# Modulation panels moved from attention's in-projection to the last layer's DeltaNet core

## The reference, cut to what matters

```
for i in range(DEPTH):
    m_ctx = split(silu(c_ctx) @ ada_w[i] + ada_b[i], 6)     # ada_w[i]: 1024 x 6144
    m_lat = split(silu(c) @ ada_w[i] + ada_b[i], 6)
    h = modulate(x, norm_mix[i], m[0], m[1])
    x = x + m[2] * mixer_i(h)
    h = modulate(x, norm_ffn[i], m[3], m[4])
    x = x + m[5] * channel_mixer_i(h)
```

## Time and profile before

| | |
|---|---|
| median of 3 runs | 2366.56 us (2366.43 to 2367.58) |
| profiled execution | 2363.55 us |
| its span, first to last instruction | 2361.7 us |
| PE busy | 2241.4 us, 95% |
| DVE busy | 483.8 us, 20% |
| ACT busy | 393.0 us, 17% |
| modulation matmuls (768) | 98.1 us |
| mean granted TensorE clock | 0.972 |

### The profile page before, as it was taken

One profiled execution on the slowest core, in us unless ns is written; L12 is line 12 of the kernel. 1 busy time (PEld: TensorE's weight loads), 2 busy tenths in 40 slices (PEclk: granted clock), 3 DMA queues, 4 the chain that ended last, 5 costly groups with the idle time before them and its releaser, 6 DMA issues.

```text
span 2361.7 us, 43842 instructions
## 1 busy us (share of the span) xinstructions
PE 2241.4 (95%) x19531; PEld 1614.3 (68%) x19531; DVE 483.8 (20%) x1376; ACT 393.0 (17%) x819; POOL 66.9 (3%) x109
## 2 busy tenths in 40 slices
PE   6999998999999999899998899999998889998999
PEld 4776666888888655445676588888878875454455
DVE  2234332000112400000211410002344423000002
ACT  1133223000100100000113310002143331000001
POOL 4000001000000000000000000000000000000000
PEclk8999999999999899999999899999999999999999
DMA  8967898753356499999574695414440057999991
GB/s 326 275 232 286 314 318 268 210 155 116 107 169 210 151 384 387 380 379 382 211 241 170 225 277 177 134 36 125 132 136 7 12 178 256 386 382 379 379 387 51
DMA packets 355909, 550.90 MB, mean 233 GB/s; under 512 B 11280, under 2 KB 311184, under 8 KB 343232
## 3 DMA queue, kind: packets, MB, share of 16 engines
q1 hardware_dynamic: 344352, 525.31, 64.1%
q0 software_dynamic: 5840, 18.11, 3.0%
q10 hardware_dynamic: 5536, 4.73, 0.6%
HBM read 537.64 MB, written 14.93 MB: 234 GB/s over the span
## 4 chain that ended last, share of the span: by engine, by line
PE 85%; DVE 5%; DMA 3%; SPq 3%; ACT 2%; issue 1%; ACTq 0%; DVEq 0%
PE ps L641 83%; SPq L481 3%; DMA ring<-in_moe_w_down 2%; ACT ring L1441 1%; DVE ring L1989 1%; ACT work L1441 1%; DVE ring L2007 0%; DVE work L1848 0%; PE ps L1137 0%; DVE ring L2012 0%; DVE ring L1997 0%; PE ps L1032 0%; DMA ring<-in_ada_w 0%; DVE ring L2015 0%; PE ps L667 0%
## 5 line engine op out<-in xcount | busy, mean ns | idle before, releaser
L641 PE MATMUL ps<-ring,work 128*32 128x384 f32 (+6 forms) x7752 | 700.7, 452 | 36.7 <-DMA ring<-in_moe_w_down 26.0
L641 PE MATMUL ps<-hT,ring 128*128 128x256 f32 x3200 | 714.6, 382 | 3.4 <-DVE hT L1858 3.2
L641 PEld LDWEIGHTS ps<-hT,ring 128*128 128x128 f32 x3200 | 609.4, 191 | 113.3 <-issue 12.2
L641 PEld LDWEIGHTS ps<-ring,work 128*32 128x32 f32 (+2 forms) x7752 | 340.5, 116 | 371.7 <-issue 257.0
L1441 ACT ACTIVATE work<-ps 128x256 f32<-128x256 f32 (+5 forms) x244 | 101.8, 436 | 1350.7 <-PE ps L641 1170.5
L641 PE MATMUL ps<-work,ring 128*128 128x256 f32 (+1 forms) x1344 | 289.7, 375 | 10.9 <-DVE work L2074 6.3
L641 PEld LDWEIGHTS ps<-work,ring 128*128 128x128 f32 (+1 forms) x1344 | 243.0, 188 | 47.3 <-DVE work L2074 8.0
L641 PE MATMUL ps<-ring 64*64 64x64 f32 (+1 forms) x4192 | 183.2, 230 | 18.6 <-ACT ring L1441 7.2
L641 PEld LDWEIGHTS ps<-ring 64*64 64x64 f32 x4192 | 160.7, 139 | 58.0 <-ACT ring L1441 24.2
L1441 ACT ACTIVATE ring<-ps 128x512 f32<-128x512 f32 (+3 forms) x208 | 101.6, 491 | 341.0 <-PE ps L641 329.9
L641 PE MATMUL ps<-work 128*128 128x128 f32 (+2 forms) x736 | 107.4, 297 | 4.3 <-DVE work L2194 4.2
(11 more groups left out here) (263 smaller groups left out, 948.9 us busy)
## 6 DMA issues: line engine op xcount, KB each, us to landing
ring<-in_moe_w_gu SPq DMA_DIRECT2D x96, 1536.0 KB, 16.0
ring<-in_ada_w SPq DMA_DIRECT2D x96, 1024.0 KB, 7.1
ring<-in_moe_w_down SPq DMA_DIRECT2D x48, 1536.0 KB, 16.1
ring<-in_ff_w_gu SPq DMA_DIRECT2D x88, 512.0 KB, 6.0
ring<-in_dn_w_in SPq DMA_DIRECT2D x32, 1024.0 KB, 5.4
ring<-in_moe_w_gu SPq DMA_DIRECT2D x32, 1024.0 KB, 8.8
ring<-in_ff_w_down SPq DMA_DIRECT2D x44, 512.0 KB, 7.3
ring<-in_moe_w_down SPq DMA_DIRECT2D x32, 512.0 KB, 11.6
```

Source lines behind the costliest of these rows:

```text
L641: return pe.matmul(out, lhsT, rhs, start=start, stop=stop, **kw)
```

## The change

Layer 2's in-projection gets no modulation panels. Its loop over heads keeps 16, now of groups 9 and 10. The last eight (group 11, the last third of layer 3's modulation) are computed in layer 3's own core: five behind `s_ks` of pair 0, one at place x = 3 in each of pairs 1 to 3, and the turn behind level 1 of pair 3. The sequences, and so the slots, follow.

```
-EARLY, GATES, CORE, NA_IN, NA_GATES = 8, 16, 48, 8, 16
+EARLY, GATES, CORE, NA_GATES, LATE = 8, 16, 48, 16, 8
...
     if KIND[l] == "na":
-        late = ada[EARLY + GATES + CORE:]
-        mixed = []
-        for i, u in enumerate(units):
-            mixed.append(u)
-            if 1 <= i <= NA_IN:
-                mixed.append(late[i - 1])
-        units = mixed + late[NA_IN:]
+        units += ada[EARLY + GATES + CORE:-LATE]
+    if l == DEPTH - 1:
+        units += ada[-LATE:]
     return units + [("out", i) for i in range(4)]
...
+        PANELS3 = [{1: 5}, {3: 1}, {3: 1}, {3: 1}]
...
                 def s_ks(j):
-                    if j == 0 or l == 0:
-                        pe.wait_ge(d_ar, ada_turned[0])
+                    pe.wait_ge(d_ar, ada_turned[0])
...
                 def s_z(j):
-                    if l == 0:
-                        pe.wait_ge(d_ar, ada_turned[0])
+                    pe.wait_ge(d_ar, ada_turned[0])
...
                 def panels(j, x):
-                    for _ in range(PANELS[j].get(x, 0) if l == 0 and j < PAIRS else 0):
+                    for _ in range((PANELS if l == 0 else PANELS3)[j].get(x, 0) if j < PAIRS else 0):
                         ada(0)
-                def turn(j, when):
-                    if l == 0 and j in when:
+                def turn(j, when, late):
+                    if (l == 0 and j in when) or (l > 0 and j in late):
                         pe.wait_ge(d_r0, head(l, j, 1)[2] + 1)
                         ada_turn(ZB, ROWS512(l, True))
...
                         if lev in (1, 3):
-                            turn(j, TURN_UT1 if lev == 1 else TURN_UT3)
+                            turn(j, TURN_UT1 if lev == 1 else TURN_UT3, (3,) if lev == 1 else ())
...
             def attention(l):
                     project(u[w], w % 2, hT, 2 * l if w == 0 else None)
-                    if 1 <= w <= NA_IN:
-                        ada(2, 3, ROWS512(l))
-                ada_turn(3, ROWS512(l))
...
-                    out(j, OUT_QD)
+                    out(j, OUT_QD, (3,))
...
-                            turned(j, TURN_UT1)
+                            turned(j, TURN_UT1, (3,))
...
-                ada_rows(2, ROWS512(l))
-                modulation(3)
```

More of the change, by code:

```diff
@@ L316, in trunk @@
         assert sum(sum(x.values()) for x in PANELS) == CORE
+        PANELS3 = [{1: 5}, {3: 1}, {3: 1}, {3: 1}]
+        assert sum(sum(x.values()) for x in PANELS3) == LATE
         PJ0 = {0: 0, 1: 12, 2: 20, 3: 32}
@@ L2034, in both, with out, turned @@
                         step(*head(l, j, p))
-                def out(j, when):
-                    if l == 0 and j in when:
+                def out(j, when, late=()):
+                    if (l == 0 and j in when) or (l > 0 and j in late):
                         ada_rows(0, ROWS512(l, True))
-                def turned(j, when):
-                    if l == 0 and j in when:
+                def turned(j, when, late=()):
+                    if (l == 0 and j in when) or (l > 0 and j in late):
                         modulation(ZB)
```

## The result

| | before | changed |
|---|---|---|
| median | 2366.49 us (2361.10 to 2367.58, 6 runs) | 2352.82 us (2351.50 to 2357.81, 6 runs) |
| profiled execution | 2363.55 us | 2353.04 us |
| span | 2361.7 us | 2351.2 us |
| mean granted TensorE clock | 0.972 | 0.978 |

The ratio is 0.9949 (95% interval 0.9936 to 0.9962): 12 us less, between 9 and 15. Two more comparisons of the same two kernels gave 0.9959 (0.9947 to 0.9971) and 0.9961 (0.9947 to 0.9975), about 9.5 us less. The profiled executions differ by 10.5.

The account below looks back on a forecast made before the run. TensorE's order of work was taken to bound the kernel (85% of the chain). -8.93 - 0.44 - 2.1 + 1.0 + 0.4 = -10.1 us gave 2356.5 from a median of 2366.56; range 2353.5 to 2361.0.

Parts of the forecast that it names:

- panels and turn out of layer 2's in-projection: Layer 2's in-projection is TensorE-bound, so removing eight panels saves 8.93 us and the turn's four transposes 0.44.
- core, pair 0: clock kept: Layer 3's core: five panels hold the granted clock, returning 0.77 + 1.36 = 2.1 us; lower bound 0.
- core, pair 0: five panels: Layer 3's core, behind s_ks: panels fit under the vector engine's time and cost nothing; 4.5 us without that cover.
- core, x = 3, three times: Pairs 1 to 3, between s_t of head 0 and s_tz: one panel each costs 0.34 us, 1.0 for three.
- core, the turn: Pair 3 behind level 1: four transposes, 0.66 us in layer 0, partly under a 0.23 us ScalarE wait, cost 0.4.
- my three panels: Layer 2's in-projection: three weight panels without modulation panels between take 20.82 us, 6.94 each, used to price the saving.
- The lower price of 0.97 for each panel: Layer 2's in-projection: a modulation panel alone takes 0.97 us, giving only 7.8 saved, the lower bound to 8.93.
- The cover of pair 0: Layer 3's core: the vector engine sets the 7.61 us from s_ks to s_t of head 1; five panels fit under it.
- the equality of 7.61 in both layers: s_ks to s_t of head 1 takes 7.61 us in layer 0 with five panels and in layer 3 without.
- The caution that I took from the same page: The gate's phase is free, slow matmuls vary between runs, so the 2.1 us is uncertain; without it the gain is 8.0.
- Transfers: The eight 1 MB loads, issued as layer 3's slots free, and the output panels behind them land in time: hidden.
- The first expert's weights: Their stream ends some 9 us earlier but waits, since the next expert's first load awaits the first gate product: nothing.

Follow-up runs that it names:

- with six: Changed kernel with loads apart, six panels in pair 0's hole, none in pair 3, the turn behind the core; ratios 0.9966 and 0.9964 against the kernel before.
- the kernel with the hole filled: Kernel before plus 40 panel-shaped matmuls on constants behind s_ks of pair 0 in layer 3's core, result unused, no loads; ratio 0.9993, pair 0 27.78 us.
- the late panels left out: Changed kernel without group 11's eight panels, their loads, copy, turn and addition, ones in place of their results; ratio 0.9967 against the kernel before.
- the hole left open: Changed kernel with pair 0's five panels moved to place 3 of pair 1, so six stand there; ratio 0.9987 against the kernel before.
- loads apart: Changed kernel with the seventh and eighth late panel loads held to pairs 1 and 2, output panels to the core's tail; ratios 0.9938 and 0.9943.
- the execution with held-back loads: Kernel before, hole open, with four output panels and two first-expert loads (7 MB) waiting for s_ks of pair 0; pair 0 33.15 us, not 29.97.

## Why the prediction was right, point by point

The forecast was 2356.5 us from a median of 2366.56, 10.1 less. The measured median, 2352.8, lies 0.7 below the low end of my range; the ratio times 2366.56 gives 2354.5, inside it. By the traces ("the sums" are the few 512-column matmuls that add up squares for a norm, one such step ahead of layer 2's heads and one at the end of the core, ahead of layer 3's output projection):

| term | forecast | measured |
|---|---|---|
| panels and turn out of layer 2's in-projection | -9.37 | -9.79 |
| core, pair 0: clock kept | -2.1 | -2.2 |
| core, pair 0: five panels | 0 | 0 |
| core, pair 0: stall by the burst of loads | not in the sum | +1.7 |
| core, x = 3, three times | +1.0 | +0.7 |
| core, the turn | +0.4 | +0.64 |
| clock in the sums ahead of layer 2's heads, and in those at the end of the core | not in the sum | -0.4, -0.95 |
| sum of the rows | -10.1 | -10.3 |

The spans differ by 10.5; the 0.2 that the rows leave is spread over stages that weren't edited. That the total came out so near is luck in part: the stall of 1.7, which I had not foreseen, is made good by 1.35 of clock that I had not foreseen either, and by 0.4 more from layer 2.

**Layer 2.** Right in kind: TensorE set this stage and what left it came off. It was 0.4 more, since an unbroken weight panel is 6.91 from start to start (all but the first, which is 7.31 in both kernels) and not 6.94; my three panels still held the slower one behind a modulation panel. The lower price of 0.97 for each panel would have been too low: the weight panel behind a two-column panel is slower too (7.11 for 6.91).

**The cover of pair 0** was the step that I trusted most, for the equality of 7.61 in both layers, and it held at 7.60 with five, with six, and on constants.

**The clock.** The Trainium skill, "TensorE: Matmul & The Clock Gate", Part 1, has the gate follow how busy the engine has been. Here the traces agree: in each of the ten executions with the hole filled the 112 matmuls took 3.71, in the four with it open 4.83 to 5.17. The caution that I took from the same page was needed elsewhere. The clock varied between executions of one kernel in the sums, in the heads and behind the core, not in the hole.

**Transfers** is the step that failed, though the total hid it. I asked whether each load lands in time, and it does. I did not ask what the loads do to TensorE. Their burst cost 1.7 us, nearly all that the clock gave. The experiments show that the burst makes the stall: it moved to pair 1 with the burst, came without panels when only loads were moved in, and went when they were held apart. The traces show what TensorE waits for there: its next block of instructions, which set off late. The Trainium skill, "Runtime: NRT & Kernel Launch", Instruction fetch mechanics, says that a sequencer fetches the next block with a DMA queue of its own while it executes, mostly hidden. The traces agree on the queue (q8) and on the place, which is the same matmul in three executions; "mostly hidden" did not hold here, with 1.64 to 1.76 us at a DMA share of 1.09.

**The first expert's weights** came earlier (the last of its loads was issued 30.0 us behind the start of the output projection, and 36.0 before) and waited, as forecast: the second expert's first load went out at 1959.26, 7.68 behind the first expert's product, as before (1969.20 behind 1961.52).

**The size.** The 0.4 of clock ahead of layer 2's heads is chance: from the context transposes to the heads' first product it is 21.71 us in twelve of the 14 traces, whatever the kernel, and 22.15 in two, of which the profiled execution of the kernel before is one. The 0.95 at the end of the core is not a thing of one execution. The changed kernel took 8.97 or 8.98 us from the first sum to the output projection in all three executions, and so did the kernel with the hole filled; the one execution of the kernel before took 9.92, the two with the late panels left out or the hole left open 9.92 and 9.93, and loads apart 9.87 and 9.31. What sets it isn't shown. Much of the spread of the comparisons (9.2 to 12.1 us) may lie outside the change: the start of layer 2's in-projection, ahead of all that was edited, came between 1183.5 and 1190.1 us in the traces. What sets that stays open.

## What to carry to other kernels

When work is moved into a hole, price it by its twin, a place of the same trace where the same code already runs with such work in it: here 7.61 against 7.61 said "free" better than any sum of durations. Then ask what else the moved work lets go: slots freed in a burst are loads in a burst, and a stage of many small matmuls can lose to them what it won. Such a stage uses up its instructions fast: here 256 of them in 4.4 us (1783.38 to 1787.77 in the execution with held-back loads), where layer 2's in-projection, at 32 matmuls in 6.91 us, needs 28 (an estimate from these two numbers). Spread the loads over stages that have time, and look at the whole kernel afterwards, since a stage that ends earlier may meet the clock differently.

## What the runs showed of the hardware

- With the transfers saturated (DMA share 1.04 to 1.10; in one stop the burst ended, and the share over it is 0.50), runs of 64-column matmuls in layer 3's core stopped for 0.8 to 2.1 us without any semaphore: in six executions with a burst there, in none of the eight without. Stops of the same kind (0.24 to 1.48 us) stand in layer 0's core in 13 of the 14 traces. All 45 stand at the same place of a block of 256 TensorE instructions, 1.2 to 1.6 us behind the landing of a 16 KB packet of queue q8.
- More work took less time: 40 matmuls in a hole of 5.4 us made the pair 2.19 us shorter, by the granted clock alone (0.61 in the stretch behind the open hole, 1.00 behind the filled one).
- The clock, not the transfers, made the widest difference between executions of one kernel. With loads apart, layer 2's loop over heads took 70.12 us in one execution and 63.77 in another. In the slower one three modulation panels took twice their time, and the granted clock over 32 us was 0.77; the changed kernel has 0.95 in the same part. Timeline of PE of the slower execution, loop over heads of layer 2:

```profile
1334.98 5.30 PE L643 MATMUL ps<-ring,csil 128*2 128x512 f32 x24
```

  The same view and place of the changed kernel:

```profile
1327.20 2.76 PE L639 MATMUL ps<-ring,csil 128*2 128x512 f32 x24
```
